# Residual blocks of a hybrid decoder layer: turned by VectorE block transposes in SBUF instead of by TensorE

## The chip, the cores and the metric

The kernel runs on one core of one Trainium2 chip. The metric is the device time of one execution in microseconds; the median of several executions is compared. The engines are called by their short names in the profile: PE is TensorE, DVE is VectorE, ACT is ScalarE, POOL is GpSimd and SP is SyncE. A name with q behind it is an engine's instruction sequencer.

## The reference

One decoder layer on x of 256 rows and 2048 columns in float32: half a gated feed-forward step, a mixer, half a second feed-forward step, and a final norm. Each of the three inner stages starts with an RMS norm of x and ends by adding its product to x.

```python
for l in range(DEPTH):
    x = x + 0.5 * swiglu(rms_norm(x, ffn1_norm[l]), ffn1_w_gate[l], ffn1_w_up[l], ffn1_w_down[l])
    h = rms_norm(x, mix_norm[l])
    proj = h @ w_in[l]
...
    x = x + jnp.concatenate([y_conv, y_attn], axis=-1) @ w_out[l]
    x = x + 0.5 * swiglu(rms_norm(x, ffn2_norm[l]), ffn2_w_gate[l], ffn2_w_up[l], ffn2_w_down[l])
return rms_norm(x, final_norm)
```

y_conv is a gated causal convolution over three rows, y_attn a differential attention with eight heads of 128 columns. The feed-forward width is 5632.

## The kernel before

**Products.** Every product is made in full float32 precision out of three faster ones: both operands are split into a high and a low part in the reduced type, and PE adds hi x w_hi (L287), hi x w_lo (L288) and lo x w_hi (L289) in PSUM. The 256 rows are the stationary side, as transposed tiles xT_hi and xT_lo (128 features x 256 rows each, 16 of them), hT (hidden) or yT (mixer output). Weights stream as the moving side.

**Chunks and the ring.** SP loads weights in chunks of 256 x 512 into four buffers `raw`. A chunk is two weight tiles, for which PE runs 12 matmuls of 512 columns. ACT copies a chunk to w_hi (`high`, L488) as soon as the chunk four places before it has been used, and DVE subtracts (`low`, L678) to get w_lo. Chunk n is used by PE while step n of ACT's and DVE's programs makes chunk n+4. ACT, DVE and PE each run their instructions in the order in which they are written, so all other work of ACT and DVE is set into this sequence by hand, at a step k of a group of chunks.

**Groups.** An output of 512 columns is a group. Its chunk count is 8 where 2048 features are summed (gate and up, the mixer's input projections Q, K, V, B, C, X, and the output projection) and 22 in the down products. Banks 0 to 3 of PSUM hold the sums of two groups in turn.

**Residual groups.** The down product of the first feed-forward (`residual`, 4 groups of 22 chunks) and the output projection (4 groups of 8 chunks) add their result to x. At the last step of a group DVE scales and adds the sum and x into `turn_in` (L790), ACT takes squares of it for the next norm (L518, whose product goes to `gate` and is not used), and POOL copies it back to x (L955) and gets the gains of the norm (`gcol`, L953). At step 1 of the next group PE transposes the eight 128x128 blocks into banks 6 and 7 (`turn_drained`, L311), ACT writes them, scaled by the gain, to xT_hi (L495), and DVE subtracts to get xT_lo (L687).

**The last group of each set.** It is turned inside the next stage: after chunk 1 of the first Q projection (L445), and after chunk 1 of the second feed-forward's gate (L334). PE waits for its tiles at chunks 6 and 7 of that group (L443 and L332). Just ahead of both places DVE computes the norm's factor (`norm_factor`, a chain of small operations L710 to L716); in the mixer ACT also waits for it (L610) before its first weight copy.

**Hidden blocks.** In the feed-forward, DVE turns the 256 x 512 hidden block in `turn_in` itself: `turn_hidden(i)` issues four transposes of 32x32 blocks (L698) at each of steps 0 to 3, into `hidT`, which is another view of `gate`; ACT splits at step 4 (L502), DVE at step 5 (L705).

The steps that set the order of the last group on DVE and of its user on PE:

```python
if early and n == 1:
    early()
...
if first and second == 0:
    pe.wait_ge(turned_lo, tbx + k + 1)
...
if u == Q and k >= CD - 2:
    pe.wait_ge(turned_lo, TB_XM + k + 1)
```

Of the kernel before, what the change touches and what calls it, by code (L numbers as in the profile page):

```python
# [27 lines left out]
F32 = mybir.dt.float32  # L28
# [15 lines left out]
W = 512  # L44
# [59 lines left out]
def hybrid_block(nc, x_in, wg1, wu1, wd1, w_in, w_out, wg2, wu2, wd2, gf, columns, lambdas, out):  # L104
    ctx = ExitStack()
    with ctx:
# [81 lines left out]
        sums_taken = sem("sums_taken")  # L188
        hid_turned = sem("hid_turned")
        hid_hi = sem("hid_hi")  # L190
        hid_lo = sem("hid_lo")
# [84 lines left out]
        def _(pe):  # L276
# [33 lines left out]

            def turn_drained(tb, pair, second):  # L311

                pe.wait_ge(turned_lo, tb)
                for t in range(TT):
                    pe.wait_ge(drained[second], pair * TT + t + 1)
                    turn(turn_in, T_HIGH, t, turned)

            def turn_x(g):
# [7 lines left out]

            def gate_up(ch, pr, tbx, c, first=False, start=False, early=None):
                for second in range(2):
                    banks_free(pr + c, second)
                    for k in range(CD):  # L330
                        if first and second == 0:
                            pe.wait_ge(turned_lo, tbx + k + 1)  # L332
                        unit(ch + 2 * CD * c + CD * second, second, xT_hi, xT_lo, CD, k)
                        if early and second == 0 and k == 1:  # L334
                            early()
                        if start and second == 0 and k + 2 < XG:
                            turn_x(k + 2)

            def residual(ch, pr, tb, hi, lo, chunks, ready, order=None, final=False, early=None):

                for i in range(XG // 2):
                    for second in range(2):
                        banks_free(pr + i, second)
                        base = ch + 2 * chunks * i + chunks * second
                        whole = chunks - RING if final and i == XG // 2 - 1 and second == 1 else chunks
                        for k in range(whole):
                            if second == 0:
                                ready(k)
                            unit(base, second, hi, lo, chunks, k, order)
                            if k == 1 and second == 0 and i == 0 and early:  # L350
                                early()
                            if k == 1 and (second or i) and not final:
                                turn_drained(tb + 4 * i + 2 * second - 2, pr + i + second - 1, 1 - second)

                        for t in range(TT):
                            for k in range(whole, chunks):
                                unit(base, second, hi, lo, chunks, k, order, tiles=(t,))

            def feed_forward(ch, pr, tbx, hid, ch_down, pr_down, tb_next, start, final, early=None):
                gate_up(ch, pr, tbx, 0, first=True, start=start, early=early)  # L360
                with pe.Fori(1, GROUPS) as c:
# [73 lines left out]
            for j in range(J):  # L435
                ch, pair, hb, tb, jb = CH_MIX + 6 * CD * j, PR_MIX + 3 * j, HJ * j, TB_HEAD + HJ * j, 4 * j
                for u in (Q, K, V, B, C, X):
                    banks_free(pair + u // 2, u % 2)
                    for k in range(CD):
# [4 lines left out]
                        unit(ch + CD * u, u % 2, xT_hi, xT_lo, CD, k)  # L444
                        if u == Q and k == 1:  # L445
                            if j == 0:
                                turn_drained(TB_XM + 2 * (XG - 1), PR_DOWN1 + XG // 2 - 1, 1)
                            else:
                                turn_gated(j - 1)
                        s = CD * (u - B) + k  # L450
# [17 lines left out]
            def ready(k):  # L468
# [4 lines left out]
                if k == 6:  # L473
                    pe.wait_ge(conv_lo, 2)
            residual(CH_OUT, PR_OUT, TB_X2, yT_hi, yT_lo, CD, order=OUT_ORDER, ready=ready,
                     early=lambda: turn_gated(J - 1))
            feed_forward(CH_FFN2, PR_FFN2, TB_X2, GROUPS, CH_DOWN2, PR_DOWN2, None, False, True,
                         early=lambda: turn_drained(TB_X2 + 2 * (XG - 1), PR_OUT + XG // 2 - 1, 1))


        @block.scalar
        def _(act):
# [28 lines left out]

            def squares(src, q, waits, last=False):

                if not (isinstance(q, int) and q == 0):
                    act.wait_ge(sums_taken, q)
                for t in range(TT):
                    waits(t)
                    a = act.activation(gate[:, t], src[:, t], ACT.Square, accum_out=sq[:, t:t + 1])  # L518
                    if last:
# [12 lines left out]
            def gate_up(ch, pr, hid, norm, c, first=False, start=False, early=None):  # L532
                base = ch + 2 * CD * c
                for n in range(2 * CD):
# [11 lines left out]
                    high(base + n + RING, n % RING)  # L546
                    if early and n == 1:
                        early()
                    if start and 2 <= n < 2 + XG:
                        g = n - 2  # L550
                        squares(x[:, :, g * W:(g + 1) * W], g, lambda t: None)
                    if not first and n == 4:
                        split_hidden(hid, c - 1)

            def split_drained(tb, r, g):

                act.wait_ge(gcol_ready, r + g + 1)
                split_x(tb + 2 * g, T_HIGH, gcol, xT_hi, BT * g)

            def residual(ch, pr, tb, q, r, chunks, final, hid=None, early=None):  # L560
                for i in range(XG // 2):
                    for second in range(2):
                        g = i * 2 + second
                        end = final and g == XG - 1
                        for k in range(chunks):
                            if not (end and k >= chunks - RING):
                                high(ch + chunks * g + k + RING, (chunks * g + k) % RING)
                            if early and g == 0:
                                early(k)
                            if k == 1 and g > 0 and not final:  # L570
                                split_drained(tb, r, g - 1)
                            if hid is not None and g == 0 and k == 4:
                                split_hidden(hid, GROUPS - 1)
                        squares(turn_in, q + g, lambda t: act.wait_ge(drained[second], (pr + i) * TT + t + 1), last=end)

# [35 lines left out]
            for j in range(J):  # L611
                ch, pair, hb, tb, jb = CH_MIX + 6 * CD * j, PR_MIX + 3 * j, HJ * j, TB_HEAD + HJ * j, 4 * j
                for u in (Q, K, V, B, C, X):
                    for k in range(CD):
# [6 lines left out]
                        for h in range(HJ):  # L621
# [7 lines left out]
                            if s == 5 * h + 8:  # L629
                                act.wait_ge(turned, tb + h + 1)  # L630
                                act.activation(yT_hi[:, bass.ds(j * HJ + (KD // 2 + h), 1), :].rearrange("p a n -> p (a n)"),
# [16 lines left out]
                        high(ch + CD * u + k + RING, k % RING)  # L648
                        if u == Q and k == 1:
                            if j == 0:  # L650
                                split_drained(TB_XM, 0, XG - 1)
                            else:
                                split_gated(j - 1)
                        if u == Q and k == 3 and j > 0:
# [16 lines left out]
        def _(dve):  # L671
# [20 lines left out]

            def turn_hidden(i):

# [4 lines left out]
                if i == 3:  # L699
                    v.then_inc(hid_turned, 1)  # L700

# [48 lines left out]
            def gate_up(ch, pr, hid, c, first=False, start=False, early=None):  # L750
                base = ch + 2 * CD * c
                for n in range(2 * CD):
# [8 lines left out]
                    low(base + n + RING, n % RING)  # L761
                    if early and n == 1:
                        early()
                    if start and 2 <= n < 2 + XG:
# [10 lines left out]
            def split_drained(tb, g):  # L775

                split_x(tb + 2 * g, T_HIGH, gcol, xT_hi, xT_lo, BT * g)

            def residual(ch, pr, tb, q, r, chunks, factor, final, hid=None, early=None):
                for i in range(XG // 2):  # L780
                    for second in range(2):
                        g = i * 2 + second
                        end = final and g == XG - 1
                        for k in range(chunks):
# [12 lines left out]
                            if early and g == 0:  # L797
                                early(k)
                            if k == 1 and g > 0 and not final:
                                split_drained(tb, g - 1)  # L800
                            if hid is not None and g == 0:
# [62 lines left out]
            for j in range(J):  # L864
                ch, pair, hb, tb, jb = CH_MIX + 6 * CD * j, PR_MIX + 3 * j, HJ * j, TB_HEAD + HJ * j, 4 * j
                for u in (Q, K, V, B, C, X):
                    for k in range(CD):
# [46 lines left out]
                        low(ch + CD * u + k + RING, k % RING)  # L914
                        if u == Q and k == 1:
                            if j == 0:
                                split_drained(TB_XM, XG - 1)
                            else:
                                convolve(j - 1)
                        if u == Q and k == 4 and j > 0:  # L920
# [5 lines left out]

            gate_up(CH_FFN2, PR_FFN2, GROUPS, 0, first=True, early=lambda: split_drained(TB_X2, XG - 1))
            with dve.Fori(1, GROUPS) as c:
# [88 lines left out]
```

## Time and profile before

| | |
|---|---|
| time, median of 3 runs | 1855.92 us (1855.12 to 1856.23) |
| the profiled execution | 1855.46 us |
| its span, first to last instruction | 1853.2 us |
| PE busy | 1830.8 us, 99% |
| PE weight loads busy | 1509.3 us, 81% |
| DVE busy | 1127.1 us, 61% |
| ACT busy | 834.9 us, 45% |
| POOL busy | 25.8 us, 1% |
| DMA | 350.17 MB, mean 189 GB/s |

The busy shares are averages over the whole span. Matmuls are pipelined: each has a record of some 390 ns, but they start some 230 ns apart, so starts have to be read and not durations. Idle time of an engine off the chain costs nothing. What a waiting engine's queue holds behind the wait does not show in the shares, but in the timelines.

### The profile page before, as it was taken

To read this page: it belongs to the slowest core of one execution; us is meant where nothing else is said; L and a number is where in the kernel's file an instruction comes from. 1 tells how busy PE (TensorE), PEld (TensorE's weight loads), DVE (VectorE), ACT (ScalarE), POOL (GpSimd) and SP (SyncE) were. 2 spreads that over 40 slices of the span, in tenths; PEclk is the share of its full clock that TensorE was granted. 3 is DMA by queue.
4 is the path that set the end of the run, shared out by engine and by line. 5 is a ranking of instruction groups with operands and counts; after the bars stand their busy time and mean duration, and the time that the engine had idled before them with its cause. 6 is when DMAs were issued, how large, how long until landed. Compare 5 with 4: busy or idle time off the path is not lost.

```text
span 1853.2 us, 23330 instructions
## 1 busy us (share of the span) xinstructions
PE 1830.8 (99%) x8184; PEld 1509.3 (81%) x8184; DVE 1127.1 (61%) x1519; ACT 834.9 (45%) x993; POOL 25.8 (1%) x36
## 2 busy tenths in 40 slices
PE   7999999999999999999999999999999999999997
PEld 6888888888888888888888788888888888888886
DVE  5666666666655554556657755666666666654554
ACT  6444444444444443545445444444444444443443
POOL 0000000000000000000000000000000000000000
PEclk9999999999999999999999999999999999999999
DMA  7666666666655555655654556666666666655553
GB/s 257 198 193 192 194 192 192 193 192 193 193 193 185 190 187 189 191 171 163 191 181 152 178 182 189 195 193 193 193 193 192 192 193 190 192 195 193 191 191 130
DMA packets 181163, 350.17 MB, mean 189 GB/s; under 512 B 10864, under 2 KB 10992, under 8 KB 180976
## 3 DMA queue, kind: packets, MB, share of 16 engines
q1 hardware_dynamic: 180672, 348.17, 61.3%
q0 software_dynamic: 144, 1.05, 0.1%
q8 instruction: 37, 0.61, 0.1%
q10 hardware_dynamic: 288, 0.17, 0.1%
q14 instruction: 22, 0.18, 0.0%
HBM read 347.25 MB, written 2.10 MB: 189 GB/s over the span
## 4 chain that ended last, share of the span: by engine, by line
PE 98%; DVE 1%; DMA 1%; issue 0%; ACT 0%; SPq 0%; ACTq 0%; DVEq 0%
PE bank L287 32%; PE bank L288 32%; PE bank L289 32%; PE bank L306 1%; DMA x<-in_x_dram 1%; PE bank L395 0%; PE bank L412 0%; DVE w_lo L678 0%; PE bank L381 0%; DVE conv L820 0%; PE bank L403 0%; PE bank L420 0%; ACT gate L518 0%; DVE turn_in L790 0%; DVE conv L823 0%
## 5 line engine op out<-in xcount | busy, mean ns | idle before, releaser
L678 DVE TENSOR_TENSOR w_lo<-raw,w_hi 128x1024 fp32r<-128x1024 f32 x656 | 809.9, 1236 | 691.9 <-ACT w_hi L488 689.7
L488 ACT ACTIVATE w_hi<-raw 128x1024 fp32r<-128x1024 f32 x656 | 694.3, 1059 | 883.7 <-PE bank L289 880.0
L287 PE MATMUL bank<-w_hi,xT_hi 128*128 128x512 f32 x1792 | 701.7, 392 | 0.0
L289 PE MATMUL bank<-w_hi,xT_lo 128*128 128x512 f32 x1792 | 698.0, 389 | 0.0
L288 PE MATMUL bank<-w_lo,xT_hi 128*128 128x512 f32 x1792 | 697.7, 389 | 0.0
L287 PEld LDWEIGHTS bank<-w_hi,xT_hi 128*128 128x128 f32 x1792 | 336.7, 188 | 71.2 <-issue 2.7
L289 PEld LDWEIGHTS bank<-w_hi,xT_lo 128*128 128x128 f32 x1792 | 336.6, 188 | 70.5
L288 PEld LDWEIGHTS bank<-w_lo,xT_hi 128*128 128x128 f32 x1792 | 336.8, 188 | 69.1
L287 PE MATMUL bank<-w_hi,hT_hi 128*128 128x512 f32 x704 | 276.2, 392 | 0.0
L288 PE MATMUL bank<-w_lo,hT_hi 128*128 128x512 f32 x704 | 276.2, 392 | 0.0
L289 PE MATMUL bank<-w_hi,hT_lo 128*128 128x512 f32 x704 | 274.4, 390 | 0.0
L698 DVE STREAM_TRANSPOSE gate<-turn_in 32x256 f32<-32x256 f32 x352 | 153.4, 436 | 5.7
L287 PEld LDWEIGHTS bank<-w_hi,hT_hi 128*128 128x128 f32 x704 | 132.2, 188 | 29.5
L289 PEld LDWEIGHTS bank<-w_hi,hT_lo 128*128 128x128 f32 x704 | 132.2, 188 | 29.5
L288 PEld LDWEIGHTS bank<-w_lo,hT_hi 128*128 128x128 f32 x704 | 132.3, 188 | 27.5
L287 PE MATMUL bank<-w_hi,yT_hi 128*128 128x512 f32 x128 | 50.7, 396 | 2.5 <-issue 1.4
L289 PE MATMUL bank<-w_hi,yT_lo 128*128 128x512 f32 x128 | 50.3, 393 | 0.0
L288 PE MATMUL bank<-w_lo,yT_hi 128*128 128x512 f32 x128 | 49.9, 390 | 0.0
L544 ACT ACTIVATE gate<-bank,rstd 128x512 f32<-128x512 f32 x44 | 30.1, 689 | 19.4 <-DVE hT_lo L705 10.4
L502 ACT ACTIVATE hT_hi<-gate 128x1024 f32 (+1 forms) x22 | 23.4, 1064 | 30.2 <-DVE gate L698 30.2
L759 DVE SCALAR_TENSOR_TENSOR turn_in<-bank,rstd,gate 128x512 f32<-128x512 f32 x44 | 30.9, 743 | 0.0
L287 PEld LDWEIGHTS bank<-w_hi,yT_hi 128*128 128x128 f32 x128 | 24.1, 188 | 7.9 <-issue 1.6
(95 smaller groups left out, 418.0 us busy)
## 6 DMA issues: line engine op xcount, KB each, us to landing
raw<-in_ffn_w_gate_dram SPq DMA_DIRECT2D x176, 512.0 KB, 4.4
raw<-in_ffn_w_up_dram SPq DMA_DIRECT2D x176, 512.0 KB, 4.1
raw<-in_ffn_w_down_dram SPq DMA_DIRECT2D x176, 512.0 KB, 3.7
raw<-in_w_in_dram SPq DMA_DIRECT2D x96, 512.0 KB, 4.3
raw<-in_w_out_dram SPq DMA_DIRECT2D x32, 512.0 KB, 3.7
x<-in_x_dram SPq DMA_DIRECT2D x4, 512.0 KB, 10.6
out_dram<-x SPq DMA_DIRECT2D x8, 256.0 KB, 2.6
gfin<-in_final_norm_dram POOLq DMA_DIRECT2D x1, 1024.0 KB, 9.6
```

Source lines behind the costliest of these rows:

```text
L287: pe.matmul(acc, hi[:, kt, ts], w_hi[slot][:, kk], start=(k == 0 and kk == 0), stop=False)
L288: pe.matmul(acc, hi[:, kt, ts], w_lo[slot][:, kk], start=False, stop=False)
L289: mm = pe.matmul(acc, lo[:, kt, ts], w_hi[slot][:, kk], start=False, stop=(k == chunks - 1 and kk == KC - 1))
L306: mm = pe.transpose(bank[banks[b]][:, kk * SEQ + t * P:kk * SEQ + (t + 1) * P], src[:, t, blk * P:(blk + 1) * P], ident[:])
L488: act.activation(w_hi[slot][:], raw[slot][:], ACT.Copy).then_inc(hi_ready, 1)
L502: act.activation(hT_hi[:, bass.ds(BT * c, BT), :], hidT, ACT.Copy).then_inc(hid_hi, 1)
L544: act.activation(gate[:, t], bank[t][:], ACT.Silu, scale=rstd[:, t:t + 1])\
L678: dve.tensor_tensor(w_lo[slot][:], raw[slot][:], w_hi[slot][:].bitcast(F32), ALU.subtract)\
L698: v = dve.transpose(dst[32 * j:32 * j + 32, :, :, i], src[32 * i:32 * i + 32, :, :, j])
L759: dve.scalar_tensor_tensor(out=turn_in[:, t], in0=bank[2 + t][:], scalar=rstd[:, t:t + 1], in1=gate[:, t], op0=ALU.mult, op1=ALU.mult).the ...
```

## The change

Residual blocks no longer go through PE. DVE turns `turn_in` with the same helper as the hidden blocks, at steps 0 to 3 of the next group, into `hidT` (the view of `gate`). ACT writes xT_hi from there at step 4, DVE writes xT_lo at step 5. For the last group of a set these are steps of the next stage's first group; its users on PE, at chunks 6 and 7, keep their waits. As `gate` is now in use, the squares' unused product goes to banks 4 and 5. The count that the head transposes wait for is lowered by the eight that PE no longer makes.

```diff
@@ tensor
-            def turn_drained(tb, pair, second):
-
-                pe.wait_ge(turned_lo, tb)
-                for t in range(TT):
-                    pe.wait_ge(drained[second], pair * TT + t + 1)
-                    turn(turn_in, T_HIGH, t, turned)
...
-                            if k == 1 and (second or i) and not final:
-                                turn_drained(tb + 4 * i + 2 * second - 2, pr + i + second - 1, 1 - second)
...
-                        if u == Q and k == 1:
-                            if j == 0:
-                                turn_drained(TB_XM + 2 * (XG - 1), PR_DOWN1 + XG // 2 - 1, 1)
-                            else:
-                                turn_gated(j - 1)
+                        if u == Q and k == 1 and j > 0:
+                            turn_gated(j - 1)
...
-            feed_forward(CH_FFN2, PR_FFN2, TB_X2, GROUPS, CH_DOWN2, PR_DOWN2, None, False, True,
-                         early=lambda: turn_drained(TB_X2 + 2 * (XG - 1), PR_OUT + XG // 2 - 1, 1))
+            feed_forward(CH_FFN2, PR_FFN2, TB_X2, GROUPS, CH_DOWN2, PR_DOWN2, None, False, True)
@@ scalar
-            def squares(src, q, waits, last=False):
+            def squares(src, q, waits, junk, last=False):
...
-                    a = act.activation(gate[:, t], src[:, t], ACT.Square, accum_out=sq[:, t:t + 1])
+                    a = act.activation(junk[t], src[:, t], ACT.Square, accum_out=sq[:, t:t + 1])
...
-                    if early and n == 1:
+                    if early and n == 4:
                         early()
...
                 act.wait_ge(gcol_ready, r + g + 1)
-                split_x(tb + 2 * g, T_HIGH, gcol, xT_hi, BT * g)
+                act.wait_ge(block_turned, r + g + 1)
+                for b in range(BT):
+                    a = act.activation(xT_hi[:, BT * g + b], hidT[:, b], ACT.Copy, scale=gcol[:, b:b + 1])
+                    if b % 2:
+                        a.then_inc(turned_hi, 1)
...
-                            if k == 1 and g > 0 and not final:
+                            if k == 4 and g > 0 and not final:
                                 split_drained(tb, r, g - 1)
...
-                        squares(turn_in, q + g, lambda t: act.wait_ge(drained[second], (pr + i) * TT + t + 1), last=end)
+                        squares(turn_in, q + g, lambda t: act.wait_ge(drained[second], (pr + i) * TT + t + 1),
+                                (bank[4][:], bank[5][:]), last=end)
...
-                                act.wait_ge(turned, tb + h + 1)
+                                act.wait_ge(turned, tb - 2 * XG + h + 1)
...
+                        if u == Q and k == 4 and j == 0:
+                            split_drained(TB_XM, 0, XG - 1)
@@ vector
-            def turn_hidden(i):
+            def turn_hidden(i, done=hid_turned):
...
-                split_x(tb + 2 * g, T_HIGH, gcol, xT_hi, xT_lo, BT * g)
+                for b in range(BT):
+                    if b % 2 == 0:
+                        dve.wait_ge(turned_hi, tb + 2 * g + b // 2 + 1)
+                    v = dve.scalar_tensor_tensor(out=xT_lo[:, BT * g + b], in0=hidT[:, b], scalar=gcol[:, b:b + 1],
+                                                 in1=xT_hi[:, BT * g + b].bitcast(F32), op0=ALU.mult, op1=ALU.subtract)
+                    if b % 2:
+                        v.then_inc(turned_lo, 1)
+
+            def turn_drained(k, pair, second, tb, g):
+
+                if k == 0:
+                    dve.wait_ge(drained[second], (pair + 1) * TT)
+                if k < 4:
+                    turn_hidden(k, block_turned)
+                if k == 5:
+                    split_drained(tb, g)
...
-                            if k == 1 and g > 0 and not final:
-                                split_drained(tb, g - 1)
+                            if g > 0 and not final:
+                                turn_drained(k, pr + (g - 1) // 2, 1 - second, tb, g - 1)
...
+                        if u == Q and j == 0:
+                            turn_drained(k, PR_DOWN1 + XG // 2 - 1, 1, TB_XM, XG - 1)
...
-            gate_up(CH_FFN2, PR_FFN2, GROUPS, 0, first=True, early=lambda: split_drained(TB_X2, XG - 1))
+            gate_up(CH_FFN2, PR_FFN2, GROUPS, 0, first=True, early=lambda k: turn_drained(k, PR_OUT + XG // 2 - 1, 1, TB_X2, XG - 1))
```

## Rows read from the trace of the kernel before

**Rows 1.** The page's part 4: the chain that ended last, by line.
```profile
PE bank L287 32%; PE bank L288 32%; PE bank L289 32%; PE bank L306 1%; DMA x<-in_x_dram 1%; PE bank L395 0%; PE bank L412 0%; DVE w_lo L678 0%; PE bank L381 0%; DVE conv L820 0%; PE bank L403 0%; PE bank L420 0%; ACT gate L518 0%; DVE turn_in L790 0%; DVE conv L823 0%
```

**Rows 2.** Groups by line and form, PE: count, busy us, mean ns, idle before.
```profile
L306 PE MATMUL bank<-ident,turn_in 128*128 128x128 f32 x64 | 8.3, 272 | 0.0
```

**Rows 3.** Timeline of ACT, down product: start us, duration, instruction, idle before it.
```profile
561.42 1.06 ACT L488 ACTIVATE w_hi<-raw 128x1024 fp32r<-128x1024 f32 x1 [1.69 <-PE bank L289]
...
565.04 1.06 ACT L488 ACTIVATE w_hi<-raw 128x1024 fp32r<-128x1024 f32 x1 [1.11 <-PE bank L289]
567.79 1.06 ACT L488 ACTIVATE w_hi<-raw 128x1024 fp32r<-128x1024 f32 x1 [1.69 <-PE bank L289]
```

**Rows 4.** Timeline of DVE, first feed-forward, hidden block turned.
```profile
66.99 1.23 DVE L678 TENSOR_TENSOR w_lo<-raw,w_hi 128x1024 fp32r<-128x1024 f32 x1
...
70.04 1.23 DVE L678 TENSOR_TENSOR w_lo<-raw,w_hi 128x1024 fp32r<-128x1024 f32 x1
...
74.35 1.79 DVE L698 STREAM_TRANSPOSE gate<-turn_in 32x256 f32<-32x256 f32 x4
```

**Rows 5.** Timeline of ACT at the same place.
```profile
76.30 1.07 ACT L502 ACTIVATE hT_hi<-gate 128x1024 f32 x1 [1.39 <-DVE gate L698]
```

**Rows 6.** Timeline of PE, first Q projection: first matmul of chunk 6.
```profile
756.83 0.39 PE L287 MATMUL bank<-w_hi,xT_hi 128*128 128x512 f32 x1
```

**Rows 7.** Timelines of DVE (first three) and ACT, start of the mixer.
```profile
746.65 2.36 DVE L678 TENSOR_TENSOR w_lo<-raw,w_hi 128x1024 fp32r<-128x1024 f32 x2 [0.66 <-ACT w_hi L488]
748.93 1.65 DVE L687 SCALAR_TENSOR_TENSOR xT_lo<-bank,gcol,xT_hi 128x256 fp32r<-128x256 f32 x4
...
752.74 1.23 DVE L678 TENSOR_TENSOR w_lo<-raw,w_hi 128x1024 fp32r<-128x1024 f32 x1 [1.02 <-ACT w_hi L488]
...
747.38 1.54 ACT L495 ACTIVATE xT_hi<-bank,gcol 128x256 fp32r<-128x256 f32 x4
748.93 1.06 ACT L488 ACTIVATE w_hi<-raw 128x1024 fp32r<-128x1024 f32 x1
751.65 1.06 ACT L488 ACTIVATE w_hi<-raw 128x1024 fp32r<-128x1024 f32 x1 [1.66 <-PE bank L289]
```

**Rows 8.** Groups by line and form, DVE and ACT: operations of 128x256 with sources in SBUF.
```profile
L820 DVE SCALAR_TENSOR_TENSOR conv<-upad,cw,conv 128x256 f32<-128x256 f32 x16 | 6.7, 481 | 0.1
...
L642 ACT ACTIVATE probs<-probs,negmax 128x256 f32<-128x256 f32 x16 | 7.9, 494 | 0.0
```

**Rows 9.** Timelines around the second gate/up: DVE, then chunk 6 on PE.
```profile
1121.58 1.28 DVE L790 SCALAR_TENSOR_TENSOR turn_in<-bank,x 128x512 f32<-128x512 f32 x2
1123.19 1.97 DVE L678 TENSOR_TENSOR w_lo<-raw,w_hi 128x1024 fp32r<-128x1024 f32 x1 [0.34 <-ACT w_hi L488]
...
1127.87 2.36 DVE L678 TENSOR_TENSOR w_lo<-raw,w_hi 128x1024 fp32r<-128x1024 f32 x2
...
1139.09 0.39 PE L287 MATMUL bank<-w_hi,xT_hi 128*128 128x512 f32 x1
```

**Rows 10.** Timelines of PE (DVE once): the start, and a gap in the output projection.
```profile
11.96 1.97 PE L306 MATMUL bank<-ident,x 128*128 128x128 f32 x8 [4.64 <-DMA x<-in_x_dram]
...
14.58 0.63 PE L289 MATMUL bank<-w_hi,xT_lo 128*128 128x512 f32 x1
...
16.05 0.39 PE L287 MATMUL bank<-w_hi,xT_hi 128*128 128x512 f32 x1
...
17.43 1.03 PE L306 MATMUL bank<-ident,x 128*128 128x128 f32 x8
...
1046.39 1.22 DVE L831 TENSOR_TENSOR yT_lo<-conv,yT_hi 128x1024 fp32r<-128x1024 f32 x1
...
1047.66 0.50 PE L287 MATMUL bank<-w_hi,yT_hi 128*128 128x512 f32 x1 [1.10 <-DVE yT_lo L831]
...
1048.22 0.39 PE L289 MATMUL bank<-w_hi,yT_lo 128*128 128x512 f32 x1
```

**Rows 11.** The view of cores: span and mean granted clock.
```profile
core 0: 1853.2 us, clock 0.998
```

## What is predicted, before the changed kernel is run

> **What bounds the kernel now.** I read the chain that ended last first: the three products of the split matmul (L287, L288, L289) are 32% of the span each [rows 1]. So nothing outside TensorE is worth anything unless it makes TensorE wait, and anything taken off TensorE's own queue is a gain in full. Then I looked at the matmuls by form for what the change removes: 64 transposes of residual blocks [rows 2]. Last I laid the timelines of TensorE, DVE and ACT side by side at the three places where the blocks are used: a middle group of a residual product, the start of the input projections of the mixer, and the start of the second gate/up product. The reader is to see there how late DVE is when each place begins.
>
> One TensorE chunk (two weight tiles, 12 matmuls) lasts 2.72 us in the stages fed by xT (ACT's copies at 748.93 and 751.65, one for each chunk, [rows 7]) and 2.75 us in the down product (565.04 to 567.79, [rows 3]). The weight path is a ring of four: ACT can make w_hi of chunk n+4 only when chunk n has been used, and DVE then subtracts to w_lo. DVE's own busy share is not near its limit, but its queue is in order, and that is what the change leans on.
>
> **Removed: TensorE's transposes.** A transpose has a record of 272 ns [rows 2], but records overlap. What eight of them cost the path is read from ACT's weight copies, one for each chunk: 3.62 us apart over the transposes (561.42 to 565.04), 2.75 us otherwise [rows 3]. So eight cost 0.87 us, and the eight residual groups that are turned (four after the first feed-forward, four after the output projection) give back 8 x 0.87 = 7.0 us. Nothing hides any of it: TensorE does not idle there.
>
> The Trainium skill (VectorE: DVE Perf Modes, The three transpose paths, and its rules for kernel authors) speaks against this change: it says to use TensorE for a 128x128 transpose when PSUM will do as the destination, and gives 390 ns against 311 ns for bf16 on the two engines; by 390 ns the 64 would give back an estimated 25 us. The trace has 0.11 us for each on TensorE's path, and 1.79 us x 4 / 8 = 0.9 us for each on DVE [rows 3, 4]; I take the rows.
>
> **Added: DVE block transposes.** The same helper already turns the hidden blocks, so its price is known: four instructions take 1.79 us, and a weight subtraction with its four transposes behind it takes 3.05 us (66.99 to 70.04, [rows 4]). A group needs four such steps, 7.2 us of DVE work. In the groups inside a residual product no product waits for these blocks before the next stage, so only the ring can be hurt. In the output projection a group of eight chunks lasts 22.0 us; DVE's work in it is four steps of 3.05, four more subtractions at 1.14 (two of them fill the 2.28 us up to the split at 748.93, [rows 7]), the split 1.57, the two drains 1.28, 0.75 for the subtraction that runs beside POOL's copy (1.97 against 1.23 us), and 0.2 for the small sum: 20.6 us [rows 7, 9]. It fits, with 1.4 us to spare. Following it step by step, the last w_lo of the four is ready about 4 us before its chunk is due, so I cost these groups at nothing on TensorE; that cover goes if DVE's steps grow by some 1.4 us in a group. But DVE ends each group some 1.3 us later than before, because the split now stands behind the sixth weight copy, and ACT makes that copy only after its own split. I carry 1.4 us of lateness into the next stage.
>
> **Moved: the last group of each set.** Here is the cost. Chunks 6 and 7 of the next stage read these very blocks and wait for them (L443, L332). Before, the blocks were turned after chunk 1 and split straight from PSUM. Now the last split stands on DVE behind the subtraction of step 5, and four steps of transposes come before it. From the start of DVE's subtraction in step 0:
> - four steps of 3.05 us = 12.20 [rows 4];
> - the last transpose to ACT's start, 74.35 + 1.79 = 76.14 to 76.30: 0.16 [rows 4, 5];
> - ACT's four copies, 747.38 to 748.93: 1.55 [rows 7]. They now read SBUF: an activation of this size from SBUF is 494 ns [rows 8], and four from PSUM fit in 1.54 us, started 0.39 apart, so at most 0.1 more;
> - the weight copy of step 5, which comes next in ACT's queue, to the start of DVE's subtraction, 751.65 to 752.74: 1.09 [rows 7];
> - that subtraction to the next operation: 1.14 [rows 7];
> - two of the four split operations, some 0.39 us apart (1.65 for four) and 0.48 long: 0.87 [rows 7]; from SBUF such an operation is 481 ns too (L820, [rows 8]);
> - DVE to TensorE, 1047.61 to 1047.66: 0.05 [rows 10].
> Sum 17.06 us.
>
> Mixer: DVE's step 0 begins at 746.65 [rows 7], late because the norm factor and ACT's exponential stand before it; the blocks are there at 763.7. Chunk 6 began at 756.83 [rows 6], without the transposes 755.96. Stall 7.7 us. Second gate/up: step 0 began at 1127.87, again behind the norm factor [rows 9], so 1144.9, and 1146.3 with the 1.4 us carried in. Chunk 6 began at 1139.09, without the transposes 1138.22. Stall 8.1 us (6.7 without the lateness). Behind both waits on TensorE stand all later chunks; the ring catches up during the stall, so nothing more is lost there, and nothing is given back either, as the work is all TensorE's.
>
> **The clock.** A stall of this length may also slow what follows. At the start TensorE idles 4.64 us, and then runs at half pace: eight transposes take 1.97 us instead of 1.03, and a matmul's record is 0.63 us at 14.58 and 0.39 at 16.05 [rows 10]; the change lies at about 15.7. That is 3.7 us from 11.96 at the lower level (1.2 GHz) and a loss of 1.85 us. The mean granted clock of 0.998 over the span [rows 11] is a loss of some 3.7 us in all, so nothing else in the span ran low for long. After a gap of 1.10 us at 1047.66 the matmuls are at 0.39 us again by 1048.22 [rows 10]. Between 1.1 and 4.64 us the trace has no gap before fast work; 7.7 and 8.1 us are beyond the longer one. I take the drop, 1.85 us each, 3.7 us; the bounds are 0 and, as one start says little of where a recovery falls, about twice that. The Trainium skill (TensorE: Matmul & The Clock Gate, Part 1) says the half-rate state is the default and only activity releases it, so an idle TensorE falls back; by that rule the term stays in, and the trace agrees at its start.
>
> **Small edits.** Squares now go to PSUM banks 4 and 5, which are idle then; ACT reads SBUF as before, and I cost it at nothing (they lie beside TensorE, except the last two in the tail, some tenths of a microsecond at most either way). POOL's copy of the gains waits for a later split, but is wanted only a group later. The shifted count for the head transposes (L630) changes no order.
>
> **Sum.** -7.0 + 7.7 + 8.1 + 3.7 = +12.5 us. The profiled execution took 1855.46 us (span 1853.2, 2.3 around it), 0.46 below the median of the runs. So 1868.0 us.
>
> **Rivals.**
> 1. The stalls come, but the clock does not fall: +8.8, 1864.3 us. For it: the 1.10 us gap left it alone. Against it: the start.
> 2. The stalls are shorter, because DVE starts its steps nearer to TensorE's pace. Even with no queue at all the split stands behind the copy and the subtraction of step 5, which need the end of chunk 5: 0.26 to ACT's start, then 1.09 + 1.14 + 0.87 + 0.05 = 3.4 us each, too short for the clock by the trace. 6.8 - 7.0: 1855.3 us, no change. Against it: DVE's lateness of 6 to 7 us at both places is in the rows.
> 3. Faster. TensorE is never held at chunk 6; the mechanism is that the blocks arrive in time, the place L443 and L332, and the gain is all of 7.0: 1848.5 us. It decides from where the two stalls together are under 7.0 us, 3.5 each; the floor above of 3.4 leaves nearly no room.
> 4. A removed transpose is worth its record, 64 x 0.272 = 17.4 us [rows 2], not 7.0: +2.1, 1857.6 us. The spacing of ACT's copies speaks against it. The skill's 390 ns would go further this way.
> 5. DVE becomes the bound in the output projection: three groups that each run past 22.0 us by a microsecond or two, or the clock takes longer to recover: 1870 to 1873 us.
>
> **How the numbers follow.** Forecast 0.64, rival 1 0.17, rival 2 0.03, rival 3 0.02, rival 4 0.02, rival 5 0.12. The range takes in rival 1 with shorter stalls (the 1.4 us of lateness may be absent) and the lower part of rival 5: 1862.5 to 1871.5. Faster by over 0.2% (3.7 us, about what a measurement can tell): 0.03; within: 0.04, from rivals 2 and 4; slower: 0.93.
>
> **What would show it.** After: no L306 on turn_in; 128 more DVE transposes on turn_in; in the waits, TensorE waits twice for xT_lo, 7 to 8 us each, at chunk 6 of the mixer's first projection and of the second gate/up; matmul records of 0.63 us for some microseconds behind each; mean clock about 0.996; no TensorE wait for w_lo in the output projection. Chunks just after a residual group's start 3.62 us apart no more. It is wrong if DVE starts its steps earlier than said, if the split operations take turns other than in the queue order, or if the pace holds after an idle of 8 us.

## The result

| | before | after |
|---|---|---|
| time, median | 1855.78 us (4 runs) | 1868.26 us (4 runs, 1867.20 to 1869.27) |
| ratio | | 1.0067, 95% interval 1.0050 to 1.0085 |
| profiled execution | 1855.46 us, span 1853.2 | 1869.27 us, span 1866.9 |

The change makes the kernel 12.5 us slower. The page of the changed kernel, busy times and the chain by engine (before, TensorE's three products had 32% of the span each, [rows 1]):

```profile
PE 1830.2 (98%) x8120; PEld 1507.0 (81%) x8120; DVE 1181.9 (63%) x1647; ACT 836.4 (45%) x993; POOL 34.2 (2%) x36
...
PE 92%; DVE 6%; ACT 1%; DMA 1%; issue 0%; SPq 0%; ACTq 0%; DVEq 0%
PE bank L288 30%; PE bank L289 30%; PE bank L290 30%; DVE w_lo L668 2%; DVE gate L688 2%; DMA x<-in_x_dram 1%; ACT w_hi L474 0%; ACT xT_hi L546 0%; PE bank L385 0%; PE bank L307 0%; DVE xT_lo L770 0%; PE bank L402 0%; DVE turn_in L795 0%; PE bank L371 0%; DVE conv L825 0%
```

TensorE has its 64 transposes less, and DVE is 54.8 us busier for 128 more transposes. But DVE's busy share of 63% says nothing of the loss. What does is that DVE now has 6% of the chain: its weight subtraction and its transposes stand in it. The view of waits says where, for TensorE:

```profile
PE bank L288 <- DVE xT_lo L770: 14.9, 2, 7.5
PE bank L307 <- DMA x<-in_x_dram: 9.5, 2, 5.0
PE bank L288 <- issue: 1.4, 1, 1.4
PE bank L288 <- DVE yT_lo L836: 1.1, 1, 1.1
```

(In each row: total idle us, number of waits, the longest.) Two waits for xT_lo are new; the other three rows were there before. The first stands at chunk 6 of the mixer's first Q projection. Its place on the timelines, DVE first, then ACT, then TensorE (start us, duration, line, instruction, idle before it):

```profile
743.75 1.23 DVE L668 TENSOR_TENSOR w_lo<-raw,w_hi 128x1024 fp32r<-128x1024 f32 x1 [0.66 <-ACT w_hi L474]
744.89 1.77 DVE L688 STREAM_TRANSPOSE gate<-turn_in 32x256 f32<-32x256 f32 x4
746.68 1.23 DVE L668 TENSOR_TENSOR w_lo<-raw,w_hi 128x1024 fp32r<-128x1024 f32 x1
...
754.05 1.79 DVE L688 STREAM_TRANSPOSE gate<-turn_in 32x256 f32<-32x256 f32 x4
755.87 1.22 DVE L668 TENSOR_TENSOR w_lo<-raw,w_hi 128x1024 fp32r<-128x1024 f32 x1
758.62 1.23 DVE L668 TENSOR_TENSOR w_lo<-raw,w_hi 128x1024 fp32r<-128x1024 f32 x1 [1.52 <-ACT w_hi L474]
759.76 1.67 DVE L770 SCALAR_TENSOR_TENSOR xT_lo<-gate,gcol,xT_hi 128x256 fp32r<-128x256 f32 x4
...
755.93 1.71 ACT L546 ACTIVATE xT_hi<-gate,gcol 128x256 fp32r<-128x256 f32 x4 [4.32 <-DVE gate L688]
757.54 1.04 ACT L474 ACTIVATE w_hi<-raw 128x1024 fp32r<-128x1024 f32 x1
...
752.78 0.39 PE L290 MATMUL bank<-w_hi,xT_lo 128*128 128x512 f32 x1
760.69 0.80 PE L288 MATMUL bank<-w_hi,xT_hi 128*128 128x512 f32 x1 [7.52 <-DVE xT_lo L770]
761.28 0.63 PE L289 MATMUL bank<-w_lo,xT_hi 128*128 128x512 f32 x1
...
766.40 0.56 PE L289 MATMUL bank<-w_lo,xT_hi 128*128 128x512 f32 x1
766.81 0.39 PE L290 MATMUL bank<-w_hi,xT_lo 128*128 128x512 f32 x1
767.04 0.40 PE L288 MATMUL bank<-w_hi,xT_hi 128*128 128x512 f32 x1
```

From DVE's step 0 at 743.75 to TensorE's restart at 760.69 it is 16.94 us; the queue is the one foreseen, step by step. ACT stands idle for 4.32 us until the last transpose is done, DVE idles 1.52 us in front of step 5 because ACT's copy for it stands behind ACT's own split, and only then comes DVE's split. The lost time is start to start, 760.69 - 752.78 = 7.91, less the usual 0.23: 7.7 us. Behind it 15 matmuls take 767.04 - 760.69 = 6.35 us instead of 3.4, with records of 0.63 us: 2.9 us more. The view by stretch (busy PE, PEld, DVE, ACT, POOL; granted clock; DMA share; GB/s) gives the clock that goes with them, half of the full one; the mean of 0.73 over the wait says that it had fallen before TensorE restarted:

```profile
753.00:760.50 7.50, 0.17 (x1) 0.00 (x0) 5.88 (x9) 2.65 (x5) 0.00 (x0) 0.73 0.61 193
760.50:766.50 6.00, 5.81 (x14) 4.55 (x15) 0.93 (x3) 0.22 (x1) 0.00 (x0) 0.50 0.32 90
```

The view of cores has the mean clock over the span, 0.992 where it was 0.998 [rows 11]:

```profile
core 0: 1866.9 us, clock 0.992
```

The second gate/up is alike: DVE's step 0, and TensorE around the wait.

```profile
1132.93 1.23 DVE L668 TENSOR_TENSOR w_lo<-raw,w_hi 128x1024 fp32r<-128x1024 f32 x1
...
1142.13 0.39 PE L290 MATMUL bank<-w_hi,xT_lo 128*128 128x512 f32 x1
1149.87 0.80 PE L288 MATMUL bank<-w_hi,xT_hi 128*128 128x512 f32 x1 [7.35 <-DVE xT_lo L770]
...
1155.59 0.53 PE L289 MATMUL bank<-w_lo,xT_hi 128*128 128x512 f32 x1
1155.96 0.40 PE L290 MATMUL bank<-w_hi,xT_lo 128*128 128x512 f32 x1
```

Again 16.94 us from step 0 to the restart; 1149.87 - 1142.13 - 0.23 = 7.5 us lost, and 2.9 us in the slow stretch. The gain shows in ACT's weight copies at the place of [rows 3], now 2.75 us apart where they were 3.62:

```profile
561.16 1.06 ACT L474 ACTIVATE w_hi<-raw 128x1024 fp32r<-128x1024 f32 x1 [1.68 <-PE bank L290]
563.91 1.06 ACT L474 ACTIVATE w_hi<-raw 128x1024 fp32r<-128x1024 f32 x1 [1.69 <-PE bank L290]
```

The account of the profiled execution: -8 x 0.87 + 7.7 + 7.5 + 2 x 2.9 = +14.0 us, against 13.8 measured (1869.27 - 1855.46). It is the slowest of the four and has the lowest mean clock, 0.992; the execution of 1868.84 us has 0.993, those of 1867.67 and 1867.20 have 0.995. So the slow clock seems to have cost less in the others, which have no trace.

### The profile page after: what moved, and what is told of

The parts are those of the page before. It is cut to its first block, busy times and chain, and to the rows that moved or that the text cites. A ratio compares the mean times of both kernels' runs of the same rounds, so it can differ in the third digit from the quotient of the medians.

```text
span 1866.9 us, 23322 instructions
## 1 busy us (share of the span) xinstructions
PE 1830.2 (98%) x8120; PEld 1507.0 (81%) x8120; DVE 1181.9 (63%) x1647; ACT 836.4 (45%) x993; POOL 34.2 (2%) x36
## 4 chain that ended last, share of the span: by engine, by line
PE 92%; DVE 6%; ACT 1%; DMA 1%; issue 0%; SPq 0%; ACTq 0%; DVEq 0%
PE bank L288 30%; PE bank L289 30%; PE bank L290 30%; DVE w_lo L668 2%; DVE gate L688 2%; DMA x<-in_x_dram 1%; ACT w_hi L474 0%; ACT xT_hi L546 0%; PE bank L385 0%; PE bank L307 0%; DVE xT_lo L770 0%; PE bank L402 0%; DVE turn_in L795 0%; PE bank L371 0%; DVE conv L825 0%
## 5 line engine op out<-in xcount | busy, mean ns | idle before, releaser
L688 DVE STREAM_TRANSPOSE gate<-turn_in 32x256 f32<-32x256 f32 x480 | 209.1, 436 | 7.8
```

The source lines that it names most:

```text
L688: v = dve.transpose(dst[32 * j:32 * j + 32, :, :, i], src[32 * i:32 * i + 32, :, :, j])
```

## Experiments

All times are medians; the kernel before ran beside each of them on the same chip, with medians from 1855.57 to 1855.77 us.

### e1_last_pe: the last groups back on TensorE

On TensorE the mixer's edit is shown; the second feed-forward's first gate gets the like. ACT and DVE split from PSUM after step 1, as before.

```diff
-                        if u == Q and k == 1 and j > 0:
-                            turn_gated(j - 1)
+                        if u == Q and k == 1:
+                            if j == 0:
+                                turn_drained(TB_XM + 2 * (XG - 1), PR_DOWN1 + XG // 2 - 1, 1)
+                            else:
+                                turn_gated(j - 1)
...
+                        if u == Q and k == 1 and j == 0:
+                            split_x(TB_XM + 2 * (XG - 1), T_HIGH, gcol, xT_hi, xT_lo, BT * (XG - 1))
```

> The last group of each set goes back to TensorE (turned after chunk 1 of the next stage), the six groups inside the residual products stay with VectorE. Theory (the whole loss is the two waits at chunk 6 and the slow clock behind them; the inner groups are free): TensorE waits for nothing at chunk 6, 6 x 0.87 = 5.2 us are gained, 1850.5 us. Rival (the transposes load VectorE, and the inner groups of the output projection cost TensorE too, or the SBUF path itself is slower): the time stays above the kernel before, 1856 us or more. Rival (a transpose is worth its record of 0.27 us): 48 x 0.27 = 13 us gained, 1843 us.

Measured: 1850.81 us (9 runs), ratio 0.9974 to before (0.9964 to 0.9984). TensorE's waits hold none for xT_lo:

```profile
PE bank L307 <- DMA x<-in_x_dram: 9.8, 2, 5.1
PE bank L288 <- issue: 1.4, 1, 1.4
PE bank L288 <- DVE yT_lo L854: 1.1, 1, 1.1
```

The theory's figure was 1850.5. So the six inner groups give back 5.0 us, 0.83 us each, against 0.87 expected, and all of the loss belongs to the two last groups. Both rivals fall.

### e2_mix_pe: only the mixer's group back on TensorE

The same edit at the mixer alone; the second gate/up keeps the changed kernel's.

```diff
+                            if j == 0:
+                                turn_drained(TB_XM + 2 * (XG - 1), PR_DOWN1 + XG // 2 - 1, 1)
```

> Only the last group before the mixer goes back to TensorE; the one before the second gate/up stays with VectorE. Theory: seven groups give back 6.1 us, one stall of 7.5 us stays and one slow stretch of 5.9 us at the lower clock (2.9 us lost): 1855.8 + 4.3 = 1860.1 us, one wait for xT_lo. Rival (the two stalls are not of the same kind, the mixer's is the one that matters): below 1857 us.

Measured: 1859.31 us (10 runs), ratio 1.0019 (1.0010 to 1.0029); one wait for xT_lo of 7.32 us. Between 1850.81 and 1859.31 lies one last group: 8.5 us, where 7.5 + 2.9 lost and 0.87 gained would give 9.5. Between 1859.31 and 1868.26 lies the mixer's: 9.0 us against 9.7. The traces have the full amounts: from TensorE's first transposes of x at full pace (at 17.43 us in [rows 10], here at 17.34) to the end of the last matmul it is 1820.6 us in e1_last_pe, 1830.1 here and 1839.9 in the changed kernel, steps of 9.5 and 9.8. So the two are of one kind. That the medians show 1.0 and 0.7 us less is not explained; most executions without a trace have a higher mean clock than the profiled one (here 0.996 or 0.997 in eight of ten, against 0.995), so a shorter slow stretch would fit.

### e3_split4: the split one step earlier

The last group of each set gets last=4, all others keep 5.

```diff
-                if k == 5:
+                if k == last:
                     split_drained(tb, g)
```

> As the changed kernel, but for the last group of each set VectorE's split stands behind the subtraction of step 4 instead of step 5, so it no longer waits for the end of chunk 5 or for ScalarE's copy behind its own split. Theory: each stall is shorter by about 2.7 us (ScalarE's four copies 1.6 and the 1.1 from its copy to the subtraction go), 5.0 and 4.8 us. If the clock falls again after 5 us, with about 2.9 us lost each: 1868.3 - 5.4 = 1862.9 us. If it does not fall at that length: 1857.1 us. Rival (the stall is the transposes' own length, not the queue behind step 5): no shorter stall, 1868 us.

Measured: 1863.32 us (4 runs), ratio 1.0041 (1.0026 to 1.0057). The idle times are 4.77 and 4.58 us where they were 7.52 and 7.35, 5.5 us less together, and the time is 4.9 us less. TensorE after the first of them:

```profile
758.50 0.80 PE L288 MATMUL bank<-w_hi,xT_hi 128*128 128x512 f32 x1 [4.77 <-DVE xT_lo L770]
759.09 0.63 PE L289 MATMUL bank<-w_lo,xT_hi 128*128 128x512 f32 x1
```

So 2.8 us of each stall come from one line's place in the queue, not from the transposes, and an idle of 4.8 us still slows the clock.

### e6_best: the last group turned as early as it fits

Eight transposes at step 0, four at each of steps 1 and 2, both splits at step 3, the norm factor after them at step 4; ACT waits for that factor only where it first scales. In the mixer three more small operations move with the norm factor, two of which had waited for ACT's exponential.

```diff
+            def turn_last(k, tb):
+                if k == 0:
+                    turn_hidden(0, block_turned)
+                if k < 3:
+                    turn_hidden(k + 1, block_turned)
+                if k == 3:
+                    split_drained(tb, XG - 1)
...
-            norm_factor(3 * XG)
+            def early_x2(k):
+                turn_last(k, TB_X2)
+                if k == 4:
+                    norm_factor(3 * XG)
```

> As the changed kernel, but VectorE turns the last group in steps 0 to 2 (eight transposes at step 0, four each at steps 1 and 2), ScalarE and VectorE split at step 3, and the norm factor is computed at step 4; ScalarE waits for it only where it first scales by it. All eight groups stay with VectorE. Theory (the stall is the sum of what stands ahead of the split in VectorE's queue): step 0 begins 3.4 to 4.3 us into the stage and the first tiles are ready 13.1 us later, 16.5 to 17.4 against the 16.3 us at which chunk 6 is due: stalls of 0.2 to 1.1 us, no slow clock: 1855.8 - 7.0 + 1.3 = 1850.1 us. Rival (the transposes hold TensorE by another way): waits of several us remain and the time stays above 1855 us.

Measured: 1851.31 us (10 runs), ratio 0.9976 (0.9967 to 0.9986). TensorE waits 1.57 and 0.58 us, and runs at full pace after both; the first:

```profile
754.21 0.50 PE L288 MATMUL bank<-w_hi,xT_hi 128*128 128x512 f32 x1 [1.57 <-DVE xT_lo L771]
754.55 0.39 PE L289 MATMUL bank<-w_lo,xT_hi 128*128 128x512 f32 x1
```

The stall follows the queue. DVE does as much as in the changed kernel, in another order, and the kernel is 17 us faster.

### e9_first_early: the first transposes ahead of step 0

In e6_best DVE idled 1.71 us before step 0 of the mixer. This one moves the first four transposes of either last group into the end of the residual product:

```diff
+                                if g == XG - 1 and not final:
+                                    dve.wait_ge(drained[second], (pr + i + 1) * TT)
+                                    turn_hidden(0, block_turned)
...
-                if k == 0:
-                    turn_hidden(0, block_turned)
```

> As e6_best, but the first four of VectorE's transposes of the last group are issued right behind the drain of its last sum, ahead of the last weight subtraction of the residual product, where VectorE idled for 1.7 us before step 0. Theory: the blocks are ready 1.6 to 1.8 us earlier, so the two waits of 1.6 and 0.6 us left in e6_best go (under 0.3 us in all), 2.2 to 2.5 us are gained: 1848.9 us. Rival (the end of the residual product has no room either, and the late subtraction or sum holds something else): 1851 us, or a new wait of TensorE.

Measured: 1849.24 us (5 runs), ratio 0.9964 (0.9951 to 0.9978). DVE at the seam to the mixer:

```profile
737.18 1.28 DVE L803 SCALAR_TENSOR_TENSOR turn_in<-bank,x 128x512 f32<-128x512 f32 x2
738.49 1.78 DVE L689 STREAM_TRANSPOSE gate<-turn_in 32x256 f32<-32x256 f32 x4
740.29 1.23 DVE L669 TENSOR_TENSOR w_lo<-raw,w_hi 128x1024 fp32r<-128x1024 f32 x1
741.43 0.15 DVE L713 TENSOR_TENSOR ssum<-ssum,sq 128x2 f32<-128x2 f32 x1
742.54 1.23 DVE L669 TENSOR_TENSOR w_lo<-raw,w_hi 128x1024 fp32r<-128x1024 f32 x1 [0.95 <-ACT w_hi L474]
```

The transposes fill what was idle, and TensorE has no wait for xT_lo any more. 6.4 of the 7.0 us are kept (1855.66 - 1849.24). Like e1_last_pe and e6_best it beats both kernels, and it is the fastest of the three.

### e10_split3: the norm factor back in front

e6_best with the norm factor's move undone; at the mixer likewise, with the three operations that had moved with it:

```diff
-            def early_x2(k):
-                turn_last(k, TB_X2)
-                if k == 4:
-                    norm_factor(3 * XG)
+            norm_factor(3 * XG)
```

> As e6_best, but the norm factor is back at its old place, ahead of step 0. Theory: VectorE's step 0 begins 1.9 us (mixer) and 2.8 us (second gate/up) later, so TensorE's waits grow to idle times of about 3.5 and 3.3 us. If an idle of 3.4 us does not slow the clock: 1851.3 + 4.7 = 1856.0 us. If it does, with 2.9 us lost each: 1861.8 us. Rival (the place of the norm factor does not matter): 1851 us.

Measured: 1859.55 us (10 runs, 1857.60 to 1861.16), ratio 1.0020 (1.0010 to 1.0029). The idle times are 3.51 and 3.32 us, as worked out, and both are followed by slow matmuls; the second one's stretch is short:

```profile
1141.01 0.80 PE L288 MATMUL bank<-w_hi,xT_hi 128*128 128x512 f32 x1 [3.32 <-DVE xT_lo L770]
...
1143.74 0.56 PE L288 MATMUL bank<-w_hi,xT_hi 128*128 128x512 f32 x1
1144.13 0.39 PE L289 MATMUL bank<-w_lo,xT_hi 128*128 128x512 f32 x1
```

8.2 us more than e6_best, for twelve small operations on two numbers a row at each place (2.6 us of DVE time at the second; at the mixer also the other three). The figure lies between the two that were expected: the clock falls, but costs less than 2.9 us each time: the second stretch of 3.1 us costs 1.5, the first of 5.7 us costs 2.8.

### e5_norm_split4: e3_split4 with the norm factor behind the split

```diff
-            norm_factor(3 * XG)
+            def early_x2(k):
+                turn_drained(k, PR_OUT + XG // 2 - 1, 1, TB_X2, XG - 1, last=4)
+                if k == 5:
+                    norm_factor(3 * XG)
```

> As e3_split4 (split behind step 4), with the norm factor moved behind the split. Theory: the stalls of 4.9 and 4.7 us shrink by 1.9 and 2.8 us, to idle times of about 2.9 and 1.8 us. Without a slow clock: 1855.8 - 7.0 + 5.0 = 1853.8 us; with one behind the longer gap only: 1856.7 us. Rival: as e3_split4, 1863 us.

Measured: 1857.08 us (10 runs), ratio 1.0005 (0.9996 to 1.0014); the single times stand in two groups, three from 1853.7 to 1854.7 and seven from 1856.9 to 1857.6. The profiled execution is of the first group. In it an idle of 2.82 us is followed by slow matmuls and one of 1.86 us is not:

```profile
754.79 0.79 PE L288 MATMUL bank<-w_hi,xT_hi 128*128 128x512 f32 x1 [2.82 <-DVE xT_lo L771]
755.38 0.63 PE L289 MATMUL bank<-w_lo,xT_hi 128*128 128x512 f32 x1
...
1137.08 0.50 PE L288 MATMUL bank<-w_hi,xT_hi 128*128 128x512 f32 x1 [1.86 <-DVE xT_lo L771]
1137.42 0.39 PE L289 MATMUL bank<-w_lo,xT_hi 128*128 128x512 f32 x1
```

Part of its lead is the start of the program: TensorE's first transposes of x at full pace, at 17.43 us in [rows 10], stand at 15.96 here. What else the slower seven do differently has no trace. Their mean clock is 0.997 in all seven, and 0.998, 0.998 and 0.997 in the three; a longer slow stretch, or one behind the second gap as well, would fit, but was not shown.

### e8_double_pe: TensorE's transposes twice, in the kernel before

```diff
                     pe.wait_ge(drained[second], pair * TT + t + 1)
+                    turn(turn_in, T_HIGH, t, None)
                     turn(turn_in, T_HIGH, t, turned)
```

> The kernel before, with TensorE's transposes of the residual blocks issued twice (64 more of them, into the same banks). Theory (eight transposes take 0.87 us of TensorE's path): 8 x 0.87 = 7.0 us more, 1862.7 us. Rival (each is worth its record of 0.272 us): 17.4 us more, 1873 us.

Measured: 1862.30 us (5 runs), 6.6 us above the 1855.66 beside it, ratio 1.0036 (1.0023 to 1.0050). ACT's copies at the place of [rows 3] are 4.50 us apart, 2.75 + 2 x 0.87:

```profile
561.28 1.06 ACT L489 ACTIVATE w_hi<-raw 128x1024 fp32r<-128x1024 f32 x1 [1.69 <-PE bank L289]
...
565.78 1.06 ACT L489 ACTIVATE w_hi<-raw 128x1024 fp32r<-128x1024 f32 x1 [1.39 <-PE bank L289]
```

A transpose among matmuls is worth 0.10 to 0.11 us (6.6 / 64 and 0.87 / 8), not its record of 0.272.

### e7_inner_double: DVE's transposes twice in the output projection, on e1_last_pe

```diff
                 if k < 4:
+                    if tb == TB_X2:
+                        turn_again(k)
                     turn_hidden(k, block_turned)
```

> As e1_last_pe, but in the three groups inside the output projection VectorE issues its 16 transposes twice (the second set goes to an unused buffer): 7.2 us more in each group of 22.0 us, to 27.8 us of VectorE work. Theory (the inner groups are free only because 20.6 us of work fit in 22.0 us): VectorE becomes the bound there, 3 x 5.8 = 17.4 us too much, less some 4 us of lead that the weight ring holds: 12 to 18 us more than e1_last_pe, 1863 to 1869 us, and TensorE waits for w_lo in many short waits. Rival (VectorE has room, as its share of busy time of 63% suggests): under 2 us more, below 1853 us.

Measured: 1868.73 us (4 runs), 17.9 us above e1_last_pe, ratio 1.0072 to before (1.0055 to 1.0089). The inner groups are free only up to DVE's room in them; a busy share of 63% over the span hid that. In TensorE's waits a new line stands first, and one of its three waits of 1.95 us is followed, after five matmuls at full pace, by a slow stretch of some 3.3 us:

```profile
PE bank L288 <- DVE w_lo L686: 11.7, 9, 1.9
```

On TensorE's timeline:

```profile
1073.95 0.47 PE L288 MATMUL bank<-w_hi,yT_hi 128*128 128x512 f32 x1 [1.95 <-DVE w_lo L686]
...
1075.49 0.63 PE L288 MATMUL bank<-w_hi,yT_hi 128*128 128x512 f32 x1
```

Three of the five waits between 1.76 and 1.95 us are followed by such a stretch, 1.6 us lost each. With 11.7 us of waits and some 0.25 us more at each of the nine restarts that is 18.7 us. The two traces differ by 18.9 us from the first transposes of x at full pace (16.01 us here, 17.88 in e1_last_pe) to the end of the last matmul. The profiled executions differ by 16.7, as this one's start was 1.9 us shorter. The expectation had no slow clock in it, so its 12 to 18 us stand against some 14 us of waits and restarts.

### e11_squares: the squares' product into PSUM, alone

```diff
-                    a = act.activation(gate[:, t], src[:, t], ACT.Square, accum_out=sq[:, t:t + 1])
+                    a = act.activation(junk[t], src[:, t], ACT.Square, accum_out=sq[:, t:t + 1])
```

> The kernel before, with the unused product of the squares written to PSUM banks 4 and 5 instead of SBUF, and nothing else changed. Theory: it lies beside TensorE but for the last two in the tail, some 0.03 us each: 1855.7 us, no change. Rival (part of the change's effect comes from here): more than 2 us either way.

Measured: 1855.50 us (10 runs) beside 1855.57, ratio 1.0000 (0.9991 to 1.0010). This part of the change costs nothing and brings nothing.

## Why the prediction was right

Forecast 1868.0 us in a range of 1862.5 to 1871.5; measured 1868.26. The direction, the two places and the mechanism are shown by the waits, the timelines and the experiments that take each away. That the figure is 0.3 us off is in part luck, as the end of this section says. Term by term:

- **Transposes off TensorE, -7.0.** Right: 2.75 us where 3.62 stood; the doubled ones added 6.6, the best version kept 6.4 of 7.0.
- **From step 0 to the first tiles, 17.06 us.** Measured 16.94 at both places. The one row for which no twin existed, ACT's copies from SBUF, came out at 1.61 us from its start to the next copy's, against 1.55, within the 0.1 allowed.
- **Stall in the mixer, 7.7.** Measured 7.7.
- **Stall at the second gate/up, 8.1.** Measured 7.5: the term of 1.4 us for DVE's lateness was too large. DVE's step 0 stands 6.9 us behind chunk 0 (1132.93, with chunk 6 due at 1142.36, six chunks of 2.72 later) where it stood 6.0 before, so 0.9 us. The lateness comes once and does not grow from group to group: the drains, DVE's rows below, are 23.1 us apart once and then 22.0. Of those 1.1 us at the groups' ends, 0.3 are caught up before step 0, 5.98 us behind the drain (1126.95 to 1132.93) where it was 6.29 [rows 9]: late as it is, DVE no longer idles for 0.34 us ahead of the last subtraction. The collision with POOL's copy costs the same in another place: it falls on the small sum (1.01 us where it was 0.15), while the subtraction is back to 1.21 from 1.97.

```profile
1059.86 1.28 DVE L795 SCALAR_TENSOR_TENSOR turn_in<-bank,x 128x512 f32<-128x512 f32 x2
...
1082.95 1.28 DVE L795 SCALAR_TENSOR_TENSOR turn_in<-bank,x 128x512 f32<-128x512 f32 x2
...
1104.94 1.29 DVE L795 SCALAR_TENSOR_TENSOR turn_in<-bank,x 128x512 f32<-128x512 f32 x2
```

- **Clock, 1.85 each.** Right that it falls, too small: 2.9 us each. It was sized from the one slow stretch that the trace of before had, 3.7 us at the start [rows 10]. Such stretches are not of one length (last section), so one row gave no size; the bound of twice that, stated with it, was the better guide. Two readings beside this term were wrong, without weight for the sum. The trace of before does have a gap between 1.1 and 4.64 us, one of 1.41 at 1028.94, and the matmuls behind it are at 0.39 us. And the mean clock of 0.998 [rows 11] does not show the slow start, where the view by stretch reads 1.00 from 11.5 to 15.5 us beside records of 0.63; it comes from the tail, where it reads 0.50 from 1846 us on, with TensorE idle. The mean came out at 0.992 to 0.995 instead of 0.996, because the slow stretches were longer and the clock was already low for some 4 us of each wait (7.5 us at a mean of 0.73), which costs nothing.
- **Small edits, 0.** Right: for the squares by a run of their own, for the gains and the count by TensorE having no other new wait.

The miss of 0.6 us in the stall and of 2.1 us in the clock have opposite signs, and the profiled execution, from which these sizes are read, happened to be the slowest of the four; against the median the total fits better than its terms do. Rival 1 (no fall of the clock) is refuted by the granted clock of 0.50. The conditions of rivals 2 and 3 did not hold for the change as it was made, but experiments came near to both. e10_split3 has rival 2's stalls, 3.51 and 3.32 us of idle time, and shows its other step wrong: these are not too short for the clock, which fell at both, and the time was 1859.55 us and not 1855.3. e9_first_early has rival 3's blocks in time, and is faster by 6.4 us. Rival 4 falls by the doubled transposes. Rival 5's bound exists: it lies somewhere within 7.2 us more of DVE work in a group (e7_inner_double).

## What to carry to other kernels

Price work that is moved to an idle-looking engine by its place in that engine's queue at the moment when somebody waits for the result: write down what stands ahead of it from the last point at which both engines were level, and compare with the consumer's due time. Here the same DVE work cost 12.5 us or brought 6.4 us, by its order alone. Of the queue's entries ahead of the result, first move those that nobody waits for yet (here a norm factor that was wanted only at the end of the group). And a removed TensorE instruction is worth the change in the spacing of its neighbours, not its record.

## What the runs showed of the hardware

- The clock falls behind much shorter idle times than the 4.64 us of [rows 10]: behind 3.32, 3.51, 4.58, 4.77 and 7.3 to 7.5 us in each case seen, behind 2.82 us in the one case seen, behind 1.76 to 1.95 us in three of six, and there only two to five matmuls after the restart (all three in e7_inner_double, which has nine waits close together); not behind 1.57, 1.41, 1.10 or 0.58 us.
- The slow stretch lasted 3.1 us (behind 2.82 and 3.32 us), 5.2 to 5.7 us (behind 4.58, 3.51 and 4.77 us) and 6.1 us (behind 7.3 to 7.5 us); half of it is lost. At the start of the program, behind the same DMA wait, the first matmul at full pace stood between 13.9 and 17.2 us in the traces, and this alone makes executions of one kernel differ. So a fall of the clock costs 1.5 to 2.9 us here, and the length of the idle time alone does not settle it.
- Four ACT copies of 128x256 with a scale took 1.71 us from SBUF against 1.54 us from PSUM; the squares' activation of 128x512 took 0.58 us with PSUM as destination against 0.62 us with SBUF.
